# A hybrid decoder trunk: key norm and head norm by one product with the matrix of ones, 512-wide roots and reciprocals, no spread

## What is computed

```python
# x: (tokens, 1024); w_in's columns split into the LRU's input and gate, and r, k, v and three low-rank inputs
kk = (k * k_k).reshape(hs)                                  # hs = (b, t, 8 heads, 64)
kk = kk / jnp.maximum(jnp.sqrt(jnp.sum(kk * kk, axis=-1, keepdims=True)), 1e-12)
k = k * (1.0 + (a - 1.0) * k_a)
z_h = -kk
b_h = kk * a_h
# scan over the tokens: s = s * w + (s z) b + v k ;  y = s r
mu = jnp.mean(y, axis=-1, keepdims=True)
var = jnp.mean(jnp.square(y - mu), axis=-1, keepdims=True)
yn = ((y - mu) * lax.rsqrt(var + RWKV_LN_EPS)).reshape(b_, t, RWKV_WIDTH) * ln_w + ln_b
bonus = jnp.sum(r_h * k_h * r_k, axis=-1, keepdims=True) * v_h
out_b = (yn + bonus) * g
```

## Time and profile before

| What | Number |
|---|---|
| Timed runs, median (range) | 1526.19 us (1524.72 to 1531.17) |
| The profiled execution, device time | 1529.27 us |
| Its span in the trace | 1527.4 us |
| TensorE busy | 1476.6 us (97%) |
| VectorE busy | 831.5 us (54%) |
| ScalarE busy | 498.2 us (33%) |
| Granted TensorE clock, mean | 0.982 |
| Chain that ended last | PE 87%, DVE 5%, ACT 3% |

### The profile page before, as it was taken

One profiled execution on the slowest core, in us unless ns is written; L12 is line 12 of the kernel. 1 busy time (PEld: TensorE's weight loads), 2 busy tenths in 40 slices (PEclk: granted clock), 3 DMA queues, 4 the chain that ended last, 5 costly groups with the idle time before them and its releaser, 6 DMA issues.

```text
span 1527.4 us, 23163 instructions
## 1 busy us (share of the span) xinstructions
PE 1476.6 (97%) x10400; PEld 1233.3 (81%) x10400; DVE 831.5 (54%) x1026; ACT 498.2 (33%) x559; POOL 81.8 (5%) x73
## 2 busy tenths in 40 slices
PE   6999999998999999999899999999998999999996
PEld 5888878786888888888788888888887788888885
DVE  6767585757644445363765545355437645354443
ACT  6444443533322122223343332332334312122230
POOL 1000000002100000001200000000012000000001
PEclk9999999998999999999899999999998999999998
DMA  4202020201322323232122222222121323232321
GB/s 179 71 8 97 3 88 18 83 4 55 124 96 98 98 95 101 92 103 91 30 108 83 83 83 83 84 83 93 73 83 32 134 83 110 83 110 84 110 83 55
DMA packets 19587, 125.10 MB, mean 82 GB/s; under 512 B 2272, under 2 KB 2272, under 8 KB 5664
## 3 DMA queue, kind: packets, MB, share of 16 engines
q1 hardware_dynamic: 19088, 121.23, 23.1%
q0 software_dynamic: 400, 2.39, 0.4%
HBM read 121.51 MB, written 2.10 MB: 81 GB/s over the span
## 4 chain that ended last, share of the span: by engine, by line
PE 87%; DVE 5%; ACT 3%; issue 2%; DMA 1%; POOL 1%; SPq 0%; POOLq 0%; DVEq 0%
PE bank L325 22%; PE bank L331 22%; PE bank L328 22%; PE bank L599 7%; PE bank L1208 2%; PE bank L1205 2%; PE bank L1202 2%; PE bank L339 2%; ACT WH L292 1%; POOL h L457 1%; DVE hn L470 1%; DVE XL L418 1%; DMA raw<-weights 1%; PE bank L1238 1%; PE bank L1237 1%
## 5 line engine op out<-in xcount | busy, mean ns | idle before, releaser
L325 PE MATMUL bank<-XH,WH 128*128 128x512 f32 x944 | 380.8, 403 | 24.4 <-DVE XL L418 12.6
L328 PE MATMUL bank<-XL,WH 128*128 128x512 f32 x944 | 372.6, 395 | 0.0
L331 PE MATMUL bank<-XH,WL 128*128 128x512 f32 x944 | 372.3, 394 | 0.0
L298 DVE TENSOR_TENSOR WL<-raw,WH 128x2048 fp32r<-128x2048 f32 (+1 forms) x111 | 249.8, 2251 | 150.0 <-ACT WH L292 150.0
L292 ACT ACTIVATE WH<-raw 128x2048 fp32r<-128x2048 f32 (+1 forms) x111 | 208.3, 1877 | 276.7 <-DMA raw<-weights 276.7
L325 PEld LDWEIGHTS bank<-XH,WH 128*128 128x128 f32 x944 | 180.3, 191 | 66.4 <-issue 28.8
L328 PEld LDWEIGHTS bank<-XL,WH 128*128 128x128 f32 x944 | 180.4, 191 | 39.1 <-issue 2.6
L331 PEld LDWEIGHTS bank<-XH,WL 128*128 128x128 f32 x944 | 180.2, 191 | 38.6
L325 PE MATMUL bank<-AH,WH 128*128 128x512 f32 x512 | 199.4, 389 | 1.1 <-DVE AL L555 0.9
L328 PE MATMUL bank<-AL,WH 128*128 128x512 f32 x512 | 199.2, 389 | 0.0
L331 PE MATMUL bank<-AH,WL 128*128 128x512 f32 x512 | 199.2, 389 | 0.0
(11 more groups left out here) (279 smaller groups left out, 1774.6 us busy)
## 6 DMA issues: line engine op xcount, KB each, us to landing
raw<-weights SPq DMA_DIRECT2D x107, 1024.0 KB, 4.8
raw<-weights SPq DMA_DIRECT2D x8, 512.0 KB, 4.9
h<-x_fm SPq DMA_DIRECT2D x4, 512.0 KB, 8.3
out_fm<-h SPq DMA_DIRECT2D x8, 256.0 KB, 2.1
rc<-ret_const POOLq DMA_DIRECT2D x1, 1536.0 KB, 6.6
pp<-pairs POOLq DMA_DIRECT2D x4, 199.0 KB, 5.0
cst<-const SPq DMA_DIRECT2D x1, 577.0 KB, 12.1
vec<-vectors SPq DMA_DIRECT2D x1, 41.5 KB, 1.9
```

The source lines that it names most:

```text
L298: nc.vector.tensor_tensor(WL[i][:, :n], raw[i][:, :n], WH[i][:, :n], ALU.subtract).then_inc(S("w_lo"), 1)
L325: mm = pe.matmul(bank[b][:], wh, xh, start=(k == 0), stop=False)
L328: mm = pe.matmul(bank[b][:], wh, xl, start=False, stop=False)
L331: mm = pe.matmul(bank[b][:], wl, xh, start=False, stop=(k == len(xs) - 1))
```

## The change

`head_sums` becomes one product of 128 partitions with 512 columns: the matrix `heads` (ones where row and column belong to the same head) is the stationary operand and the squares are the moving one. Every partition of a head then holds the head's sum for every token, and `head_spread` goes. Floor, roots and reciprocals are 128x512, in place in two tiles that are free then (`W[11]` for the keys, `ARK` for the heads), and the two multiplications read these instead of PSUM. TensorE's waits for `kk_inv`, `yc`, `ln_inv` and `yn` in the front go with the spreads.

```diff
         def head_sums(pe, b, src, signal):
-            for t in range(TT):
-                mm = pe.matmul(bank[b][:, 2 * t:2 * t + 2], src[:, t * P:(t + 1) * P], head1,
-                               start=(t == 0), stop=(t == TT - 1), skip_group_check=True)
-            mm.then_inc(S(signal), 1)
-
-        def head_spread(pe, b, src, signal):
-            for t in range(TT):
-                for j, rows in enumerate(ROWS):
-                    mm = pe.matmul(bank[b][rows, t * P:(t + 1) * P],
-                                   src[:, 2 * t + j:2 * t + j + 1].to_broadcast([P, C]), eye,
-                                   start=True, stop=True)
-            mm.then_inc(S(signal), 1)
+            pe.matmul(bank[b][:], heads, src[:], start=True, stop=True).then_inc(S(signal), 1)
...
             if p == PAIRS:
...
                 head_sums(pe, 6, ARK, "y_var")
-                out_units(pe, use, LAST - 1, (3, 4))
-                was("ln_inv")
-                head_spread(pe, 7, lninv, "ln_spread")
-                out_units(pe, use, LAST - 1, (5, 6, 7))
-                was("yn")
+                out_units(pe, use, LAST - 1, (3, 4, 5, 6, 7))
...
                 in_unit(pe, use, "k", p, (3, KT))
-                was("ln_inv")
-                head_spread(pe, 7, lninv, "ln_spread")
             in_unit(pe, use, "r", p, (0, 4))
             need("kk_sq")
             head_sums(pe, 6, W[7], "kk_sum")
             in_unit(pe, use, "r", p, (4, KT))
-            need("kk_inv")
-            if p:
-                was("yc")
-            head_spread(pe, 5, kkinv, "kk_spread")
             in_unit(pe, use, "ax", p)
             need("rk_ready")
-            if p:
-                was("yn")
-            pe.matmul(bank[7][:], heads, W[3][:], start=True, stop=True).then_inc(S("rk_sum"), 1)
+            head_sums(pe, 7, W[3], "rk_sum")
...
-                nc.scalar.activation(lnroot[:], bank[6][:, 0:8], ACT.Sqrt, bias=epsc[:, 1:2],
-                                     scale=1.0 / C).then_inc(S("ln_root"), 1)
+                nc.scalar.activation(ARK[:], bank[6][:], ACT.Sqrt, bias=epsc[:, 1:2], scale=1.0 / C).then_inc(S("ln_root"), 1)
...
-                nc.scalar.activation(kkroot[:], kkm[:], ACT.Sqrt).then_inc(S("kk_root"), 1)
+                nc.scalar.activation(W[11][:], W[11][:], ACT.Sqrt).then_inc(S("kk_root"), 1)
...
-                was("ln_spread", "yc")
-                nc.vector.tensor_tensor(O[:], Vt[:], bank[7][:], ALU.mult).then_inc(S("yn"), 1)
+                was("ln_inv", "yc")
+                nc.vector.tensor_tensor(O[:], Vt[:], ARK[:], ALU.mult).then_inc(S("yn"), 1)
...
-                nc.vector.reciprocal(lninv[:], lnroot[:]).then_inc(S("ln_inv"), 1)
+                nc.vector.reciprocal(ARK[:], ARK[:]).then_inc(S("ln_inv"), 1)
...
-            nc.vector.tensor_scalar(kkm[:], bank[6][:, 0:8], 1e-24, None, ALU.max).then_inc(S("kk_floor"), 1)
+            nc.vector.tensor_scalar(W[11][:], bank[6][:], 1e-24, None, ALU.max).then_inc(S("kk_floor"), 1)
...
-            nc.vector.reciprocal(kkinv[:], kkroot[:]).then_inc(S("kk_inv"), 1)
+            nc.vector.reciprocal(W[11][:], W[11][:]).then_inc(S("kk_inv"), 1)
...
-            need("kk_spread")
-            nc.vector.scalar_tensor_tensor(W[11][:], W[1][:], pv(Q_KK, p), bank[5][:], ALU.mult,
+            need("kk_inv")
+            nc.vector.scalar_tensor_tensor(W[11][:], W[1][:], pv(Q_KK, p), W[11][:], ALU.mult,
                                            ALU.mult).then_inc(S("kk_ready"), 1)
```

More of the change, by code:

```diff
@@ L74 @@
     "low_rank_products": "lin_w lin_a lin_g",
-    "key_norms": "kk_sum kk_spread rk_sum",
-    "head_norms": "y_sum y_var ln_spread",
+    "key_norms": "kk_sum rk_sum",
+    "head_norms": "y_sum y_var",
     "gate_products": "gate_r gate_i",
@@ L205, in trunk_kernel @@
         BDa, BDx = ab("BDa", P), ab("BDx", P)
-        kkm, kkroot, kkinv, lnroot, lninv, PC = (ab(n, 8) for n in
-                                                 ("kkm", "kkroot", "kkinv", "lnroot", "lninv", "PC"))
+        PC = ab("PC", 8)
         ffn = Place(NORM)
@@ L242, in trunk_kernel @@
         heads = cst[:, K_HEADS:K_HEADS + P]
-        head1 = cst[:, K_HEAD1:K_HEAD1 + 2]
         ones1 = vec[:, NVEC - 1:NVEC]
@@ L662, in front_pe @@
                 was("ys")
-                pe.matmul(bank[5][:], heads, Zt[:], start=True, stop=True).then_inc(S("y_sum"), 1)
+                head_sums(pe, 5, Zt, "y_sum")
                 out_units(pe, use, LAST - 1, (1, 2))
@@ L719, in need @@
                     pe.wait_ge(*nth(name, p + 1))
-            need("z_ready", "b_ready", "kk_spread")
+            need("z_ready", "b_ready")
             by_chunk(pe, 5, W[6], W[5], "azb_t", 1)
```

## The result

The changed kernel took 1537.13 us (median of 6 runs, 1535.66 to 1538.86) against 1526.61 us of the kernel before (6 runs, 1524.72 to 1531.17). The ratio is 1.007, 95% interval 1.0059 to 1.0082: slower by 9 to 12.5 us. Forecast were 1537.0 us and +10.8; measured is +10.5. That the two agree to 0.3 us is closer than the interval allows anyone to claim.

What follows compares the result with a forecast made beforehand. TensorE, busy 97% of the span, was taken as the bound. Pair 0 +5.1, pairs 1 to 3 +5.4, their clock +1.5, behind the last pair -1.2: +10.8, or 1537.0 us on the median; range 1527 to 1544.

Steps and rivals of the forecast that it cites:

- What TensorE saves: Eight spreads of 1.22 us go, wide sums about tie with narrow ones; TensorE alone would save 10.1 us.
- The price of the reciprocal: On VectorE, a 512-column reciprocal takes 3.3 us, from a slope between small sizes giving 2.6 to 3.35.
- rival with eight steps a column: VectorE's 512-column reciprocal takes 4.3 us, slot 4.2; +17.8 us in all, 1544 us; chance 0.12.
- cheap side: Reciprocal of 2.6 us gives +6.2, 1532 us; with the clock also full everywhere, 1529 us; chance 0.22.
- Pair 0: Late split_lo holds TensorE's first ax product 3.5 us longer; half clock behind it adds 1.6; +5.1 us.
- Pairs 1 to 3: TensorE waits for key squares and rk_ready, gate_r starts 1.8 us later per pair; +5.4 us for three.
- The clock in pairs 1 to 3: Half clock behind TensorE's waits costs 1.0 us a pair, taken in half of the three; +1.5 us.
- plain-pass case: Reciprocals run at one pass, slot 0.61, no long pause in pair 0; -3.9 us, 1522 us; chance 0.05.
- count of seven reciprocals: Above the hidden part, each 0.1 us of reciprocal costs 0.7: once in pair 0, twice in each later pair.

Runs made afterwards that it cites:

- idle products: Changed kernel with 24 unread 128x512 products issued on TensorE where it waits in pair 0; 1534.58 us, +7.5 us against the kernel before.
- key norm alone: Kernel before with only the key norm made wide, head norm left narrow with its spread; 1535.07 us, ratio 1.0056.
- head norm alone: Kernel before with only the head norm made wide, key norm left narrow with its spread; 1524.26 us, ratio 0.9984.
- `split_lo` first: Changed kernel with the weight chunk's split_lo moved ahead of the key reciprocal in pair 0 only; 1531.6 us, ratio 1.0037.
- each reciprocal twice: Changed kernel with every 128x512 reciprocal preceded by a second one whose result is unused; 1566.33 us, ratio 1.0265.

## Why the prediction was right

- **What TensorE saves.** Behind the last pair, where products surround the head norm, the spread's 1.22 us came back (-1.29). Elsewhere the saving was there and turned into waits: 5.94, 3 x 0.92 and 3 x 2.38 us.
- **The price of the reciprocal.** The slope of the head row gave 3.35, I took 3.3, measured are 3.35 us. The slope of the key row gave 2.6; to side with the head row was a choice that came out right. The rival with eight steps a column (4.3 us) is out, and with it that reading of the Trainium skill's repeat count ("VectorE: DVE Perf Modes", "First, the fixed hardware budget"): the step here is 6.25 ns a column. The cheap side is out as well.
- **Pair 0.** The place was right: first product of ax +3.55 from the low-rank product on (13.65 us behind it in place of 10.10), forecast +3.5. The idle products show what the clock cost there: 2.4 us, where I counted 1.6, since the half clock lasted 12 products and not 8. For this execution the term was mis-sized; behind the same pause with the key norm alone it was 8 products, and pair 0 lost 5.0 us, near the forecast 5.1. What decides between 8 and 12 no run shows.
- **Pairs 1 to 3.** `rk_ready`'s sum starts 1.17 later (forecast 1.2) and `gate_r` 1.77 (1.8). The waits are listed as 0.92 and 2.38 us and were worked out as 1.05 and 2.65; the listed ones start at a product's modelled end, 0.39 us behind its start, and mine at 0.23 behind it. Counted my way they are 1.08 and 2.54. The 0.1 that the second lacks is the wide sum behind the first wait, which took 0.97 us and not 0.87. The wait for the convolution, forecast at 0.6, is listed as 0.36, which is 0.5 counted so. Key norm alone and head norm alone confirm that it is the key reciprocal that does the harm and that the head one only adds to it.
- **The clock in pairs 1 to 3.** Taken in half of the three at 1.0 us, it fell in one of three in the profiled execution at +1.2. So +1.5 was forecast and +1.2 came, while pair 0's clock cost 0.8 more than forecast.
- **The rivals.** The plain-pass case was run and gave its -3.9 us, though with a pause in pair 0 that I had said would not be there: without the spread TensorE stands 3.33 us, and pair 0 loses 2.5 us and not 0.9. That rival's sum was right by luck. The count of seven reciprocals held for their present length alone.

The mechanism was the forecast one, stage by stage; the last tenths are not. The forecast span of 1538.2 us was 3.3 too long, for the two profiled executions differ outside the changed stages.

What stays open is how often the clock falls behind the 2.4 us wait in runs that were not profiled; with it goes some 1 us a pair of the measured 10.5. Open too is the part of the surplus over the two norms apart that the stages do not show.

## What to carry to other kernels

Removing products from a busy TensorE pays only where the engine that feeds the next product has idle time; work out the other engine's list up to the next wait first, and price each instruction that grows from 8 to 512 columns, a reciprocal by the slope between two small sizes and not by the rate of its neighbours. Take several sizes where there are any: here the two rows of 8 columns gave 2.6 and 3.35 us. A long instruction may be nearly free in one place (the head reciprocal alone) and cost more than its length in another (pair 0, where a slot of 3.27 us became 5.0 to 6.0 with the clock): look at what stands behind it in the queue. Where it must stand, put the instructions that others wait for ahead of it, and try the engine that idles.

## What the runs showed of the hardware

- VectorE's reciprocal in float32 takes 6.25 ns a column, 3.35 us for 128x512, where a two-operand pass takes 0.69; listed ends overlap by 0.08, so the slot is 3.27.
- The granted clock fell in full-width work behind waits well under pair 0's. Behind the 2.4 us wait for `rk_ready` it fell in 1 of 3 pairs of the changed kernel, 2 of 3 with the idle products in pair 0, and 3 of 3 with `split_lo` first; behind a 1.8 us wait (key norm alone) in none of 3. With the head norm alone it fell in 2 of 3 pairs behind a wait of only 0.9 us and the eight narrow sums that follow it:

```profile
110.40:113.70 3.30, 3.30 (x10) 2.13 (x10) 2.20 (x5) 1.40 (x2) 0.00 (x0) 0.51 0.11 44
```

- It came back after 3.2 to 5.2 us of products at half rate, and with each reciprocal twice after up to 6.2 us. The Trainium skill ("TensorE: Matmul & The Clock Gate", "What's actually happening") calls the half clock the default that activity releases; the traces agree, at 0.50 for 5.2 us behind the pause of 5.94 and 1.00 where that pause was filled.
